# Three groups' score products cut into blocks, with quarters and token tiles of weight projections between them

## What is computed

```python
for i in range(DEPTH):
    h = rms_norm(x, attn_norm[i]);  proj = h @ w_in[i]
    o_a = stick_breaking_attn(sb[:, :, 0], sb[:, :, 1], sb[:, :, 2])
    o_b = causal_softmax_attn(q_m, k_m, v_m)              # latent q and k, 96 wide
    o_c = sliding_window_sink_attn(q_c, k_c, v_c, swa_sinks[i])
    o_d = moba_attn(q_d, k_d, mb[:, :, 2])                # 256 tokens: causal softmax
    groups = rms_norm(groups, group_norm[i].reshape(N_GROUPS, GROUP_WIDTH))
    x = x + groups.reshape(B, S, MIX_WIDTH) @ w_o[i]
    ...                                                   # gated MLP, per-layer embedding
```

## Time and profile before

| | |
|---|---|
| median of 3 runs | 782.57 us (782.23 to 784.56) |
| profiled execution | 782.46 us, of which the span is 780.7 us |
| PE, PEld busy | 736.5 us (94%), 646.7 us (83%) |
| POOL, ACT, DVE busy | 399.4 us, 380.6 us, 340.4 us |
| mean granted TensorE clock | 0.952 of full speed |

### The profile page before, as it was taken

How to read it: one execution, slowest core, us unless ns; L and a number is a source line. 1 busy time by engine, 2 the same in 40 slices (tenths; PEclk the granted TensorE clock), 3 DMA queues, 4 the chain that set the end, 5 groups by cost and what they waited for, 6 DMA issues and landing times.

```text
span 780.7 us, 11768 instructions
## 1 busy us (share of the span) xinstructions
PE 736.5 (94%) x4628; PEld 646.7 (83%) x4628; DVE 340.4 (44%) x542; ACT 380.6 (49%) x550; POOL 399.4 (51%) x203
## 2 busy tenths in 40 slices
PE   4899989979999999999979999899899999999997
PEld 3687977749999999998757899677699999999976
DVE  3735564443333444335174555443324443334442
ACT  4446543255545444544345485153464455455442
POOL 2320220054888887788800211002568877888863
PEclk9898987899999999999999989589999999999999
DMA  7763311136445555544519421111445655455441
GB/s 262 217 202 108 108 55 54 55 100 224 162 162 195 183 201 178 206 166 150 172 40 300 142 93 55 55 55 55 162 152 176 208 176 206 161 166 210 145 178 54
DMA packets 78883, 116.11 MB, mean 149 GB/s; under 512 B 2342, under 2 KB 66726, under 8 KB 78590
## 3 DMA queue, kind: packets, MB, share of 16 engines
q1 hardware_dynamic: 76320, 109.85, 42.4%
q10 hardware_dynamic: 2526, 5.76, 2.1%
HBM read 114.55 MB, written 1.05 MB: 148 GB/s over the span
## 4 chain that ended last, share of the span: by engine, by line
PE 85%; DVE 5%; ACT 4%; POOL 2%; DMA 2%; issue 2%; SPq 0%; DVEq 0%; POOLq 0%
PE ps L816 23%; PE ps L817 22%; PE ps L818 22%; PE ps L900 2%; DMA raw<-w_in 2%; PE ps L939 2%; PE ps L1087 2%; PE ps L857 1%; PE ps L831 1%; POOL st L384 1%; PE ps L891 1%; DVE wl L1320 1%; PE ps L932 1%; PE ps L994 1%; PE ps L1004 1%
## 5 line engine op out<-in xcount | busy, mean ns | idle before, releaser
L393 POOL TENSOR_TENSOR wl<-raw,wh 128x2048 fp32r<-128x2048 f32 (+1 forms) x78 | 349.5, 4508 | 103.1 <-ACT wh L517 103.1
L517 ACT ACTIVATE wh<-raw 128x2048 fp32r<-128x2048 f32 (+1 forms) x102 | 187.2, 1858 | 90.8 <-PE ps L818 87.8
L816 PE MATMUL ps<-hT_h,wh 128*128 128x256 f32 x768 | 219.5, 286 | 0.0
L817 PE MATMUL ps<-hT_l,wh 128*128 128x256 f32 x768 | 218.4, 284 | 0.0
L818 PE MATMUL ps<-hT_h,wl 128*128 128x256 f32 x768 | 218.4, 284 | 0.0
L816 PEld LDWEIGHTS ps<-hT_h,wh 128*128 128x128 f32 x768 | 148.8, 194 | 1.4 <-issue 0.5
L817 PEld LDWEIGHTS ps<-hT_l,wh 128*128 128x128 f32 x768 | 148.7, 194 | 0.9
L818 PEld LDWEIGHTS ps<-hT_h,wl 128*128 128x128 f32 x768 | 148.5, 193 | 0.0
L816 PE MATMUL ps<-wh,hT_h 128*128 128x256 f32 (+1 forms) x304 | 105.2, 346 | 3.3 <-ACT pr L537 1.7
L379 POOL TENSOR_SCALAR st<-st 128x2 f32<-128x2 f32 (+2 forms) x22 | 5.7, 259 | 196.4 <-ACT lat L564 109.3
L817 PE MATMUL ps<-wl,hT_h 128*128 128x256 f32 (+1 forms) x304 | 101.5, 334 | 0.0
(11 more groups left out here) (218 smaller groups left out, 902.7 us busy)
## 6 DMA issues: line engine op xcount, KB each, us to landing
raw<-w_up SPq DMA_DIRECT2D x44, 1024.0 KB, 5.1
raw<-w_down SPq DMA_DIRECT2D x22, 1024.0 KB, 4.9
raw<-w_in SPq DMA_DIRECT2D x16, 1024.0 KB, 5.4
raw<-w_o SPq DMA_DIRECT2D x6, 1024.0 KB, 5.0
raw<-ple_gate SPq DMA_DIRECT2D x6, 1024.0 KB, 4.8
raw<-w_in SPq DMA_DIRECT2D x4, 704.0 KB, 7.4
ng<-norm_gains ACTq DMA_DIRECT2D x2, 1024.0 KB, 5.1
raw<-w_o SPq DMA_DIRECT2D x4, 512.0 KB, 3.7
```

What stands on the lines that cost most here:

```text
L393: pool.tensor_tensor(wl[:, slot, 0:n], raw[:, slot, 0:n], wh[:, slot, 0:n].bitcast(F32), ALU.subtract).then_inc(ffn_l_made, 1)
L517: act.activation(wh[:, slot, 0:n], raw[:, slot, 0:n], ACT.Copy).then_inc(h_made, 1)
L816: pe.matmul(dst, a_h, b_h, start=start, stop=False, skip_group_check=True)
L817: pe.matmul(dst, a_h, b_l, start=False, stop=False, skip_group_check=True)
```

## The change

Three places on PE, in each layer. The products are the same; only their order, and where PE waits, differ. No other engine's program is changed.

```diff
@@ project is cut in project_tile for one token tile; project calls it for both
+                def project_tile(u, t, banks, col, quarters=None):
...
+                    if t == TT - 1:
+                        mm.then_inc(w_used, 1)
...
@@ scores
-                def scores(g, q, k, prev_mask, order=PAIRED):
+                def scores(g, q, k, prev_mask, order=PAIRED, between=(None, None)):
...
                     tile_1(order[0:2], 5).then_inc(F["scores_ready"], 1)
+                    if between[0]:
+                        between[0]()
 
                     pe.wait_ge(F["half_scores"], base["half_scores"] + g + 1)
                     tile_0(order[2:4]).then_inc(F["scores_ready"], 1)
+                    if between[1]:
+                        between[1]()
                     tile_1(order[2:4], 6).then_inc(F["scores_ready"], 1)
...
@@ z of the stick-breaking group, in the loop over its first two blocks b
                     mm.then_inc(F["sb_z"], 1)
+                    project_tile(M_MOBA_K, b, (2, 3), 256)
...
                 mm.then_inc(F["sb_z"], 1)
-                project(M_MOBA_K, (2, 3), 256)
...
@@ project_out takes the parts to do
-                def project_out(n, between=None, free=None):
+                def project_out(n, banks=range(4)):
...
-                scores(1, lambda h: head(qkT_moba, 0, h), lambda h: head(qkT_moba, 2, h), None)
+                scores(1, lambda h: head(qkT_moba, 0, h), lambda h: head(qkT_moba, 2, h), None,
+                       between=(lambda: project_out(0, (0,)), lambda: project_out(0, (1,))))
...
-                project_out(0, between=(3, lambda: group_T(1)), free=(2, "swaT_ready", 2))
+                pe.wait_ge(F["swaT_ready"], base["swaT_ready"] + 2)
+                project_out(0, (2,))
+                group_T(1)
+                project_out(0, (3,))
                 probs_T(1)
...
-                       GROUPED)
-                project_out(1)
+                       GROUPED, between=(lambda: project_out(1, (0,)),
+                                         lambda: project_out(1, (1,))))
+                project_out(1, (2, 3))
                 group_T(2)
```

More of the change, by code:

```diff
@@ L819, in split_product @@
                                      skip_group_check=True)
+                def project_tile(u, t, banks, col, quarters=None):
+                    slot, (_, w, k0, n) = unit(u), WIN_PARTS[u]
+                    if quarters is not None:
+                        pe.wait_ge(F[("hT_act", "hT_dve")[t]], base[("hT_act", "hT_dve")[t]] + quarters + 1)
+                    for i in range(n):
+                        k, c, tok = k0 + i, slice(i * w, (i + 1) * w), slice(t * P, (t + 1) * P)
+                        o = ps[:, banks[t], col:col + w]
+                        if u in WHOLE:
+                            mm = pe.matmul(o, hT[:, k, tok], raw[:, slot, c], start=k == 0,
+                                           stop=k == KT - 1, skip_group_check=True)
+                        else:
+                            mm = split_product(o, hT_h[:, k, tok], hT_l[:, k, tok],
+                                               wh[:, slot, c], wl[:, slot, c], k == 0,
+                                               k == KT - 1)
+                    if t == TT - 1:
+                        mm.then_inc(w_used, 1)
                 def project(u, banks, col, quarters=None):
-                    slot, (_, w, k0, n) = unit(u), WIN_PARTS[u]
                     for t in range(TT):
[L825 to L837, removed]
+                        project_tile(u, t, banks, col, quarters)
                 def project_T(u, bank):
@@ L1075, in project_out @@
                     slot = unit(U_WO + n)
-                    for b in range(4):
+                    for b in banks:
                         half, t = divmod(b, 2)
[L1078 to L1082, removed]
                         for k in range(m):
@@ L1095, in project_out @@
                             mm.then_inc(F["wo_done"], 1)
-                    mm.then_inc(w_used, 1)
+                    if b == 3:
+                        mm.then_inc(w_used, 1)
                 pe.wait_ge(F["mT_ready"], base["mT_ready"] + 4)
```

## The result

| | before | after |
|---|---|---|
| median of 4 runs each | 782.77 us (782.23 to 784.56) | 800.88 us (800.16 to 809.69) |
| profiled execution | 782.46 us (span 780.7) | 800.52 us (span 798.8) |
| mean granted TensorE clock | 0.952 | 0.95 |

The changed kernel takes 1.0266 times as long (95% interval 1.0234 to 1.0298), 18.1 us more by the profiled executions. That is slower, as forecast, and within the range of 786 to 805 us, but 5.3 us beyond the forecast of 795.3. One of the four executions of the changed kernel took 809.69 us at a mean clock of 0.938; the medians and the profiled executions differ by 18.1 us, the ratio gives 20.8.

A forecast was written before the change was run, and what follows sets the result against it. PE, busy 94% of the span, was taken to bound the kernel, with some 29 us of lost clock. Terms 12.8 + 2.6 - 1.6 - 1.0 = +12.8 us on 782.46 gave 795.3 us, range 786 to 805.

The forecast's parts named there:

- Part 1: z: MoBA keys between its blocks delay PE's next projection 4.5 and 4.9 us; +12.8 us with the low-clock restart.
- The restart: Behind PE's 8.5 us pause after z: the clock restarts low, 1.7 us a layer, 3.4 in sum.
- rival E: z: 24 products between blocks are too few, the clock falls as before; +19.6 us, 802.1 us, chance 0.07.
- Part 2: scores(1) with project_out(0) parts inside: +1.3 us taken between +0.5 and +4.2; +2.6 us for two layers.
- the forecast's case with the clock back in part 0: scores(1): clock returns in project_out(0)'s part 0, swa_T copies start 11.8 us after scores(1) began; +0.5 us.
- its low case: scores(1): clock stays low through all of it, 15.5 us; +4.2 us.
- Part 3: scores(2) with project_out(1) parts inside: one layer -2.4 us, one +0.8; -1.6 us, between -4.8 and +1.6.
- Part 4: Shifted clock falls: pv(0) saves up to 2.5 us in the second layer, may lose 1.6 in the first; -1.0 us.
- forecast A: Whole kernel: the forecast itself, +12.8 us, 795.3 us, chance 0.50.
- B: Groups 1 and 2: new pauses bring the clock down, low through both score products; +22.8 us, 805.3 us, chance 0.14.
- D: Not slower: clock up through pv(0), scores(1), scores(2), decided at pv(0)'s first product; -1.3 us, 781.2 us, chance 0.08.

The follow-up runs named there:

- part 2 alone: Kernel before, plus only parts 0 and 1 of project_out(0) in scores(1) and the swaT_ready wait right behind the transposes: 788.4 us, ratio 1.0064.
- the best kernel: Kernel before, plus project_out(0) part 0 ahead of pv(0), its part 1 mid-scores(1), and project_out(1) parts 0 and 1 in scores(2): 767.77 us, ratio 0.9799.
- the kernel with the copies moved: Changed kernel, with ACT's copies out of banks 2 and 3 ahead of the third Abs and first latent-transpose copies behind it: 791.49 us, ratio 1.011.
- the kernel with half of part 1: Changed kernel, but only one MoBA key token tile ahead of z's third block, the other behind it: 796.07 us, ratio 1.0149 against the kernel before.
- part 3 alone: Kernel before, plus only parts 0 and 1 of project_out(1) in scores(2): 778.92 us, ratio 0.9965.

## Why the prediction was right or wrong, point by point

**Part 1, the sign: right, and shown.** Its step was that the third block of z stands ahead of a fixed chain on ACT, so that 4.5 and 4.9 us of moved products are passed on to the end. Measured are 4.88 and 5.24 us. The chain is 9.38 us before and after, the pause 8.54 us where 8.5 was forecast, half the products ahead of the block gave 5.62 us, and with the copies ahead of the chain there was no pause at all. The small excess is the length of z with the keys: 11.65 us (60.54 to the end of the last mask, 71.96 + 0.23), where the working had 11.3.

**The restart: right in sum.** Forecast 1.7 a layer, measured 1.24 and 2.20, in sum 3.4 against 3.4. That the clock held in z, and with it that rival E is out, shows in the stretch of 11.5 us at 1.00. The Trainium skill (TensorE: Matmul & The Clock Gate, What's actually happening) has activity release the throttle and idleness bring it back. The runs agree on the pause (0.51 behind 8.54 us of idling). On the scores they differ as far as the busy time tells: the clock fell behind 5.20 of 5.20 us busy with 64 rows in use and stayed up with 96. But the products on 64 rows stand further apart than the busy time shows, so how busy the array really was is not settled here.

**Part 2: the mis-sized term.** The step "I take +1.3, nearer the first, since parts 0 and 1 are two chances to return" failed. The two bounds, +0.5 and +4.2 a layer, hold what was seen; the choice between them was wrong. In both layers of the changed kernel the clock stayed low through both parts (13.0 us in the first, until 525 in the second), and the cost was 2.52 and 2.44 us, 5.0 in sum for 2.6. That part 2 alone has a ratio of +5.0 us too is in part chance: its ten executions are spread over 9 us, and in the profiled one the way from scores(1) to pv(1) is 3.3 us longer in sum. The timeline of ACT shows its end: the copies of swa_T start 14.28 us after scores(1) (133.81 - 119.53), between the forecast's case with the clock back in part 0 (11.8) and its low case (15.5); the last two heads of tile 1 took 1.9 us instead of 2.7, since the clock was back at 132.5:

```profile
133.81 0.49 ACT L537 ACTIVATE qkT_swa<-ps 128x384 f32<-128x384 f32 x1 [12.30 <-PE ps L1130]
```

From there to pv(1) are 6.8 us, against the forecast 7.2. The rows that should have decided it were at hand: the clock was low *before* scores(1) began. Full rows between the blocks keep a clock that is up (pv(1) after 14.1 us in the best kernel); one that was low as the scores began returned after some 7 us at best in these runs (in the second layer of the kernel with the copies moved), and mostly after 8 us or more. That a low clock returns in one part was assumed, not read.

**Part 3: near in sum, not in its working.** -1.2 us for a forecast of -1.6. The forecast had one layer with the clock held (-2.4) and one that loses it (+0.8); measured are -0.69 and -0.54, with a short low stretch in both layers. That the mean came out close is luck. The low stretch in scores(2) became 3.6 us (from 6.7), and the norm's wait that was named is there, 0.55 us ahead of group_T(2). Alone it gives 2.7 us.

**Part 4: the sign right, the working not.** -0.5 us for -1.0. The forecast had a gain of up to 2.5 in pv(0) of the second layer and a loss of 1.6 in the first; measured are gains of 0.07 and 0.45. The low stretch from pv(0) on in the second layer did not go away but moved along with its work:

```profile
507.70:525.00 17.30, 17.30 (x55) 0.51 0.05 19
```

It follows the wait ahead of pv(0) and not a place in time, so shifting the program by 16 us gave almost nothing there.

**What no term had: +1.3 us outside the attention.** It arises at the start of the second layer: +7.55 at the first transposition of its input (399.20 → 406.75), +8.83 at the latent up-projection (425.40 → 434.23). Around the end of the wait for the input norm, the clock is low for 7.6 us in the changed kernel (404.7 to 412.3, busy for 5.55) and for 3.4 us in the one before (398.6 to 402.0, busy for 2.79), with the same instructions. Half of the difference in low busy time is 1.4 us.

Sum: 12.8 forecast; measured are +13.6 for part 1, +5.0 for part 2, -1.2 for part 3, -0.5 for part 4 and +1.3 elsewhere, 18.1 before rounding. The result lies between forecast A (+12.8) and B (+22.8). B's mechanism was half there: low through scores(1) in both layers, but not through scores(2). The prediction's own sign for B, a longer low stretch in scores(1), came: 13.0 us for 11.8. By its number E (802.1) lies nearest, but its mechanism is out, since the clock held in z. What the prediction says against E, that the clock is up in all 128-row work, is not so in its own rows: the stretch from 64.0 to 70.9 has 4 us of the keys' projection in it, and that from 139.2 to 145.9 4 us of project_out(1). D did not come, but its deciding point was badly chosen: in the first layer pv(0)'s first products did run at the full clock (1.08 us for 8, as in the kernel before), the clock fell behind them, and scores(1) was low all the same.

## What to carry to other kernels

Before independent work is put between the parts of a product, look for who waits for the last part: here it feeds 9.4 us of ACT, whose cover was the very projection that was moved ahead of it, and what was put ahead of it came out at the end. What a low stretch costs is to be read at the next wait behind it and not as half its length (1.1 us here, not 3.4). Mix products of few rows with full ones where the clock is still up, which begins by shortening the pause ahead of them; where it is already down, the mixed-in work delays the chain behind: one part was about neutral here (781.53 us), two were a loss.

## What the runs showed of the hardware

- PE can lose its clock while the profile has it 100% busy: with 64 rows of fp32 operands the same sequence falls to 0.52 and 0.50 in the two layers, with 96 rows it stays at 1.00 (781.73 and 773.01 us, one execution each). Whether the rows, the wider spacing or the longer stretch do it is open.
- Products on fewer rows were slower here: at the full clock a head with two products of 256 columns takes 0.84 us from start to start with 64 rows, 0.60 with 96.
- The same instructions may keep the clock or lose it: z of the first layer, with nothing edited ahead of it, was at 0.51 for 6.9 us in one kernel's profile and at 1.00 in another's. An edit that only shifts work can therefore gain or lose some microseconds in places that it does not touch (here +1.3 in sum, and more in the kernel with half of part 1).
- Behind a pause of 5.62 us PE lost 2.7 and 1.6 us by the low clock, behind 8.54 us 1.2 to 2.2 us: a shorter pause was not a cheaper one. Behind one of 2.75 us it lost nothing in one profile (part 3 alone) and 1.5 us in two others.
